# First layer's values and gate as seven block products, with the head in a new order

## What is computed

```
hproj = x @ w_in                    # 512 x 1024 by 1024 x 6144: q, k, v, gate
q = rope(q); k = rope(k) * DK_A ** -0.5
o = chunkwise_retention(q, k, v)    # o_n = sum over m <= n of gamma^(n-m) (q_n . k_m) v_m
o = (o - mean(o)) * rsqrt(var(o) + 1e-5)        # over the 512 values of a head
y = (o * silu(gate)) @ w_out
```

## Time and profile before

| | us |
|---|---|
| median of 3 runs | 1414.13 |
| lowest, highest | 1412.3, 1415.89 |
| the profiled execution | 1414.12 |
| its span in the trace | 1412.3 |
| PE busy | 1393.4 |
| DVE, ACT, POOL busy | 919.2, 698.8, 388.2 |

### The profile page before, as it was taken

How to read it: one execution, slowest core, us unless ns; L and a number is a source line. 1 busy time by engine, 2 the same in 40 slices (tenths; PEclk the granted TensorE clock), 3 DMA queues, 4 the chain that set the end, 5 groups by cost and what they waited for, 6 DMA issues and landing times.

```text
span 1412.3 us, 19358 instructions
## 1 busy us (share of the span) xinstructions
PE 1393.4 (99%) x7412; PEld 1203.4 (85%) x7412; DVE 919.2 (65%) x1562; ACT 698.8 (49%) x1131; POOL 388.2 (27%) x192
## 2 busy tenths in 40 slices
PE   9999999999999999999999999999999899999998
PEld 7888888888889888888888888778888899998887
DVE  6444354549961865545544479946877878789896
ACT  4323232236554533443443356648956465666554
POOL 5334254541034343343334230035314100000000
PEclk9999999999999999999999999999999999999999
DMA  7257946946533988975796557353122576446552
GB/s 292 90 194 204 296 155 164 263 115 258 188 103 129 289 235 221 312 176 157 210 302 161 162 207 284 135 193 126 64 83 75 165 184 173 128 173 213 197 187 111
DMA packets 53890, 260.26 MB, mean 184 GB/s; under 512 B 5568, under 2 KB 10304, under 8 KB 28224
## 3 DMA queue, kind: packets, MB, share of 16 engines
q1 hardware_dynamic: 37152, 163.04, 33.3%
q0 software_dynamic: 5760, 41.95, 14.9%
q10 hardware_dynamic: 10912, 54.40, 11.3%
HBM read 252.03 MB, written 91.23 MB: 243 GB/s over the span
## 4 chain that ended last, share of the span: by engine, by line
PE 89%; DVE 7%; ACT 2%; POOL 1%; issue 1%; DMA 0%; SPq 0%; DVEq 0%; ACTq 0%; POOLq 0%
PE bank L567 23%; PE bank L569 23%; PE bank L568 23%; PE bank L1176 6%; PE bank L1238 4%; PE bank L1127 3%; PE bank L1155 1%; DVE wlo L2082 1%; DVE wlo_a L2082 1%; DVE xlo L2082 1%; DVE br_lo L2082 1%; PE bank L1318 0%; PE bank L913 0%; PE bank L1015 0%; DMA stage<-in_w 0%
## 5 line engine op out<-in xcount | busy, mean ns | idle before, releaser
L724 POOL TENSOR_TENSOR wlo<-stage,whi 128x1024 fp32r<-128x1024 f32 (+2 forms) x116 | 291.9, 2543 | 544.8 <-ACT whi L1458 544.8
L1458 ACT ACTIVATE whi<-stage 128x1024 fp32r<-128x1024 f32 (+2 forms) x120 | 122.2, 1069 | 87.3 <-PE bank L569 64.3
L567 PE MATMUL bank<-xhi,whi 128*128 128x512 f32 (+1 forms) x428 | 149.3, 349 | 3.2 <-DVE xlo L2082 1.8
L569 PE MATMUL bank<-xhi,wlo 128*128 128x512 f32 (+1 forms) x428 | 148.5, 347 | 0.0
L568 PE MATMUL bank<-xlo,whi 128*128 128x512 f32 (+1 forms) x428 | 148.3, 346 | 0.0
L1461 ACT ACTIVATE whi<-stage 128x1024 fp32r<-128x1024 f32 (+2 forms) x125 | 118.0, 989 | 40.3 <-PE bank L569 29.4
L2082 DVE TENSOR_TENSOR wlo<-stage,whi 128x1024 fp32r<-128x1024 f32 x108 | 123.4, 1168 | 14.7 <-ACT whi L1461 14.7
L567 PEld LDWEIGHTS bank<-xhi,whi 128*128 128x128 f32 x428 | 81.1, 189 | 13.5 <-issue 2.2
L567 PE MATMUL bank<-whi,xhi 128*128 128x512 f32 (+1 forms) x236 | 91.4, 387 | 1.1 <-POOL wlo L724 1.1
L569 PE MATMUL bank<-whi,xlo 128*128 128x512 f32 (+1 forms) x236 | 90.4, 383 | 0.0
L568 PE MATMUL bank<-wlo,xhi 128*128 128x512 f32 (+1 forms) x236 | 90.3, 383 | 0.0
(11 more groups left out here) (451 smaller groups left out, 3943.5 us busy)
## 6 DMA issues: line engine op xcount, KB each, us to landing
stage<-in_w SPq DMA_DIRECT2D x79, 1024.0 KB, 4.9
tsum<-in_w ACTq DMA_DIRECT2D x32, 1024.0 KB, 14.5
stage<-tsum SPq DMA_DIRECT2D x32, 1024.0 KB, 4.8
tsum<-in_w POOLq DMA_DIRECT2D x16, 1024.0 KB, 10.1
tsum<-tsum POOLq DMA_DIRECT2D x16, 1024.0 KB, 10.1
stage<-in_w SPq DMA_DIRECT2D x8, 1152.0 KB, 6.3
usum<-in_w POOLq DMA_DIRECT2D x8, 1024.0 KB, 9.9
stage<-usum SPq DMA_DIRECT2D x32, 256.0 KB, 3.8
```

Of the source, the lines that this page charges most:

```text
L567: pe.matmul(dst, a_hi, b_hi, start=start, stop=False)
L569: return pe.matmul(dst, a_lo, b_hi, start=False, stop=stop)
L724: pool.tensor_tensor(lo[:, r], stage[p % 2][:, r], hi[:, r].bitcast(F32), ALU.subtract).then_inc(w_lo, 1)
L1458: act.activation(parts(p)[0][:, r], stage[p % 2][:, r], ACT.Copy).then_inc(w_hi, 1)
```

## The change

V and gate of a head are now one product of x (512 x 1024) with a 1024 x 1024 matrix: its left half is V, its right half the gate. x and the matrix are cut into 2 x 2 blocks, and seven products of 256 tokens by 512 by 512 take the place of eight. They need four sums of blocks of x (once, `operand_sum`, in head 0, from the copy of x in `xres`) and four sums of weight blocks in every head (T1 to T4: `t1`, `t3` and two more, each 128 x 2048 on DVE). The results are gathered from the products in PSUM by 12 additions a head on DVE.

A head now splits nine panels: Q, B11, K, B21, B22 by ACT and POOL, T1 to T4 by ACT and DVE. The new order on PE is

The diff, cut to the order on PE and to DVE's queue around K:

```diff
-                token_tiles(A0 + 2, n, 4, 0, lambda q: A[q][:, :], True, False,
-                            lambda q: pe.wait_ge(a_gt, 4 * h + (q + 1)), a_v)
-                token_tiles(A0 + 3, n, 4, 4, lambda q: A[q][:, :], False, True, nothing, a_v)
+                block_product(h, A_B11, X)
+                turned_product(h, AK)
+                pe.wait_ge(a_k1, 2 * h + 2)
+                block_product(h, A_B21, X, True)
 
                 pe.wait_ge(a_qklo, 4 * h + 4)
...
+            def block_product(h, j, banks, onto=False):
+
+                wh, wl = [w.rearrange("p (k n) -> p k n", k=PK) for w in a_parts(h, j)]
+                x_hi, x_lo = a_operand(j)
+                for kk in range(PK):
+                    if kk % 2 == 0:
+                        head_need(h, j, kk > 0)
+                    for a in range(2):
+                        r = slice(a * P, (a + 1) * P)
+                        last = split_dots(pe, banks[a][:, :], x_hi[:, kk, r], x_lo[:, kk, r], wh[:, kk, :], wl[:, kk, :],
+                                          kk == 0 and not onto, kk == PK - 1, onto)
+                last.then_inc(a_m, 1)
...
+                def t1():
+                    dve.wait_ge(a_ld[1], 32 * h + 32)
+                    dve.wait_ge(g_plo, 10 * h + 4)
+                    dve.tensor_tensor(s0, s1, s0, ALU.subtract).then_inc(g_sum, 1)
+
+                def t3():
+                    dve.wait_ge(a_ld[0], 32 * h + 32)
+                    dve.tensor_tensor(s1, s2, s1, ALU.subtract).then_inc(g_sum, 1)
...
+                rope(h, 0)
+                rope_lo(h, 0)
+                if h == 0:
+                    operand_sum(0)
+                    operand_sum(1)
+                    operand_sum_lo(0)
+                    dve.wait_ge(vs_s, 1)
+                    operand_sum(2)
+                    operand_sum_lo(1)
+                    dve.wait_ge(vs_s, 3)
+                    operand_sum(3)
+                    operand_sum_lo(2)
+                t1()
+                if h:
+                    t3()
+                rope(h, 1)
+                rope_lo(h, 1)
```

## The result

The changed kernel takes 1440.46 us (median; 1439.40 to 1441.44), the kernel before 1413.86 beside it: ratio 1.0187, interval 1.0169 to 1.0205. It is slower, as forecast (1419), but by 26.6 us and not by 5, and outside the range (1407 to 1427).

The account below looks back on a forecast made before the run. TensorE, 99% busy, was taken as the bound: -21.8 us of matmuls, +12.6 +0.6 +2.0 +6.5 +2.8 +0.5 of waits and +1.8 of clock give +5.0, span 1417.3; with 1.8 around it, 1419 us (8 in 10: 1407 to 1427).

Parts of the forecast that it names:

- wait 4: End of head 3: ScalarE's eight copies and GpSimd's output-product remainders make TensorE wait before T4, 2.8 us.
- What is taken away: V and gate on TensorE: 24 fewer matmuls per head, 96 in all, 21.8 us less; 72.4 us a head without waits.
- Waits 1, 2 and 3: Before the scores: K's rotation uncovered, 12.6 us; VectorE subtractions ahead of it, 0.6 plus 2.0; head 0's sums, 6.5 more.
- TensorE's clock: Behind head 0's long wait the clock drops to its lower level once, costing 1.8 us.
- The second rival: Same waits, but each of the four lowers the clock and costs 1.8 us: +5.4, 1425 us; chance 0.15.
- The hand-over: From the last transposes to the output product: the panel of its third step comes late, 0.5 us (0 to 3).
- tight T phase: Rival: T2 to T4 each wait 0.5 us in every head, and B12 is late in heads 2 and 3; 1428 us, chance 0.13.
- Covered additions: Rival: VectorE's new steps fit between GpSimd's halves, so K's rotation starts when K ends in heads 1 to 3; 1408 us, chance 0.22.

Follow-up runs that it names:

- e11: e10 with ScalarE copying the next head's B11 only behind VectorE's remainders of v, and head 0's v and fourth-sum copies ahead of B22's; 1408.00 us.
- e2: The changed kernel with ScalarE copying B22 to whi behind K's two copies to qk_hi, not ahead of them; 1444.89 us.
- e3: The changed kernel with the sum t3 moved behind K's remainders in heads 1 to 3, not ahead of K's rotation; 1442.61 us.
- e8: e7 with head 0's fourth operand sum, two remainders and t1 moved behind K's rotation on VectorE; 1421.28 us.
- e4: The changed kernel with matmuls nobody reads filling TensorE's waits before the scores and before T3 of head 3; 1435.91 us.
- e1: The changed kernel with head 3's eight copies of usum issued by SP behind its last panel load, not by ScalarE's queue; 1433.24 us.
- e5: e1 with GpSimd's four sums of the up product moved behind its weight remainders of the output product; 1433.85 us.
- e10: e9 with the first norm's second shift ahead of VectorE's remainders of the next panel, not behind them; 1416.09 us.
- e9: e8 with VectorE's steps behind K's remainders reordered, and head 3's first two output-product operands copied by ScalarE behind T4's panel; 1420.54 us.
- e7: The changed kernel with the edits of e5, e2 and e3 joined, and GpSimd's sums of heads 1 to 3 spread one behind each panel; 1421.20 us.

## Why the forecast missed, step by step

The sum missed in three places: the clock (1.8 us, measured 10.8), wait 4 (2.8, measured 11.3), and the norm, which it put at nothing without a reason (measured 3.5).

**What is taken away** held: 96 matmuls, and in e11 heads 1 and 2 take 73.6 and 74.1 us between transposes, where I had 72.4 without waits and the kernel before 77.8. In the changed kernel head 2 took 77.1, forecast some 76.

**Waits 1, 2 and 3** held in size and cause. The four gaps before the scores came to 20.0 us for a forecast of 21.7. Each step of the argument has its run: GpSimd beside K's rotation (e2, 1.27 and 2.86 down to 0.69 and 0.68), the late panel B12 with t3 in head 1 (e3, 5.0 down to 3.0), VectorE's sums ahead of K in head 0 (e8, 8.4 to none before the scores).

**TensorE's clock** failed, in its size: 1.8 us for head 0 alone, measured 10.8 us behind five waits. The step that failed reads "I take 1.8 us, since the only long idle stretch that the rows show ... was followed by the low level". From that one stretch I took both the price (the eight matmuls after it, 0.45 us each) and the number of places. The level there was read off these distances; the clock column gives 1.00 over 0 to 10 us. Behind a wait of 8.4 us in this kernel the low level cost 2.7, behind 3.0 us between 1.6 and 3.1. e4 settles it: the same waits filled with matmuls, and no head loses any.

The second rival named this mechanism, "each of the four pulls the clock down", and I gave it 0.15, since "three of them are about 3.5 us, and a gap of 1.6 us cost nothing". The prediction also says that in the kernel before "the clock never falls". That is wrong. A page that shows 9 tenths in every slice can hide a low stretch of some 7 us in a slice of 35. The trace has one, behind a wait of 2.0 us at 916.43 with 0.75 more at 918.74 (PE in time, then a window as above):

```profile
916.43 1.56 PE L913 MATMUL bank<-ident,h_tok 128*128 128x128 f32 x8 [2.00 <-DVE h_tok L2263]
918.74 0.77 PE L567 MATMUL bank<-whi,xhi 128*128 128x512 f32 x1 [0.75 <-POOL wlo L724]
```

```profile
920.00:923.00 3.00, 2.68 (x7) 1.58 (x7) 2.96 (x5) 0.00 (x0) 1.91 (x1) 0.50 0.11 19
```

The matmuls from 919.30 on stand 0.43 us apart, not 0.23. So the kernel before already held a wait shorter than the four to come and followed by the low level; the sum should have had this price in every head. The rule of the Trainium skill that I had cited against the change (TensorE: Matmul & The Clock Gate, "Why this matters for your kernels") agrees with the four waits before the scores and the one at T3; waits of 3 us that cost nothing stand in the last section.

**Wait 4** failed, by 8.5 us: 11.3 for 2.8. The term that was mis-sized is the issue of the eight copies, taken as it stood before, 5.9 us. In the new order the same issue holds ScalarE for 12.3; the DMA engines' share is 1.02 over those 12.3 us, where it was 0.85 over 240.6 to 246.5 before. Whether the busier engines are the reason is not shown. The hold itself is shown as the cause of the wait: e1 takes it away, and with it the wait at T3. GpSimd's four sums of the up product did the same to GpSimd, and its two operand remainders fell beside VectorE's remainder of T4 (e1's 7.8 us, gone in e5). The forecast had a term for those remainders (4.77 us for two) but none for the sums ahead of them.

**The first norm** was not in the sum: 3.3 us idle, 3.5 start to start. VectorE works through the output product to the norm almost without a pause (in e8 from 329.47 to 392.84 with one of 0.46). From its first step there to the second shift it takes as long as before (68.8 us for 69.1), but TensorE, with two steps of the output product done ahead of the transposes, arrives earlier relative to it, and the shift itself meets GpSimd. e10 shows the place: the shift ahead of the remainders takes 1.29, and its wait falls from 4.1 in e9 to none, with 1.8 and 0.8 in its place.

**The hand-over** took 1.7 us for 0.5. Added up: 9.0 (clock), 8.5 (wait 4), 3.5 (norm), 1.2 (hand-over), less 1.7 (the scores) are 20.5 of the 21.4 us by which the forecast was short.

The rival "tight T phase" did not occur in the changed kernel; in e7 and e8 it did, with 1 us a head, once the scores no longer waited. The range ended at 1427, just short of the 1428 that the prediction gave this rival. "Covered additions" did not occur either: the head period stayed over 74 us. Its place was real, since taking t3 out of the stretch gave head 1 its 2 us back (e3), but that gave nothing while the clock fell anyway.

## What to carry to other kernels

A product taken away next to TensorE is also a cover taken away. Price the chain behind it, and count each wait of the sizes seen here (3 us and more, once 2.0 with 0.75 behind it) twice, once as idle time and once as up to 3 us of low clock behind it. Look for the granted clock in short windows behind the waits, not only on the page. Before moving a step across a DMA issue, read how long that issue holds its engine where it will stand, with the DMA engines as busy as they will be there. Where VectorE and GpSimd meet on steps with SBUF inputs, decide by a wait who goes first: a gap that VectorE catches in one execution and misses in the next is worth 6 us of median, and shows as spread before it shows in any one trace.

## What the runs showed of the hardware

- **The clock behind a wait.** Behind a wait of 3 us the clock fell in most cases, but not in all. Scores to T1 took 9.37 us behind 2.97 (e1, head 2) and behind 3.15 (e2, head 1), and 12.3 behind 2.98 (e3, head 1). In head 2 of the changed kernel it fell only 1.9 us after the matmuls had resumed. Before the scores, 6.5 to 8.4 us of wait cost 2.0 to 2.9 in every trace that had them; ahead of T4, 7.8 us cost 1.8 (e1), and ahead of T3, 11.1 us cost 1.5 (changed kernel).
- **The shared port.** Beside GpSimd's subtractions, VectorE's steps with two SBUF inputs did not share, they stood aside: two halves of 1.2 us took 7.52, 10.54 and, of 0.64 each, 8.02 us. The Trainium skill (SBUF — State Buffer, "Who interferes with whom") states such a lock, held for a whole instruction by whoever comes first. The traces agree for one instruction (the shift, 3.40 for 1.28). Between two GpSimd instructions in a row VectorE sometimes gets in (e9) and sometimes not (e10), though it started 0.04 to 0.05 us ahead of GpSimd's by the trace in both.
- **Issues hold engines.** With the DMA engines busy throughout, eight copies of half a panel held ScalarE for 12.3 us; accumulating transfers in a row held GpSimd for 7 to 14 us each (e2), where in the kernel before, one behind each panel, GpSimd stood at most 2.6 us ahead of one. What inside the queue holds them is not shown.
